# GpSimd forms the low part of one weight piece during the pool mixer, and VectorE leaves that split out

## The reference

```python
h = modulate(rms_norm(x, norm_g[i, 1]), sh1, sc1)
y = pool_mixer(h, pool_w, pool_scale)       # window means minus h, times a 256x256 matrix per group
x = x + g1 * y
h = modulate(rms_norm(x, norm_g[i, 2]), sh2, sc2)
x = x + 0.5 * g2 * swiglu(h, ffn_w_gu[i, 1], ffn_w_down[i, 1])
```

## Time and profile before

| | |
|---|---|
| median of 3 runs | 1389.89 us (1388.96 to 1390.38) |
| the profiled execution | 1388.13 us |
| its span | 1386.5 us |
| TensorE matmuls, busy | 1328.2 us, 96% of the span |
| VectorE busy | 946.5 us, 68% |
| ScalarE busy | 643.6 us, 46% |
| GpSimd busy | 150.5 us, 11% |
| VectorE's splits of pieces (L1890) | 212, mean 2293 ns |
| mean granted clock of TensorE | 0.988 of full |

### The profile page before, as it was taken

The page is one execution under the profiler, slowest core; times in us unless marked ns, Lnnn a source line. Parts: engine busy times, 40 slices in busy tenths (PEclk is TensorE's granted clock), DMA queues, the critical chain, the costliest instruction groups (busy, mean ns, idle before and its releaser), DMA issues.

```text
span 1386.5 us, 17673 instructions
## 1 busy us (share of the span) xinstructions
PE 1328.2 (96%) x6207; PEld 1080.6 (78%) x6207; DVE 946.5 (68%) x1125; ACT 643.6 (46%) x845; POOL 150.5 (11%) x215
## 2 busy tenths in 40 slices
PE   5999999799999999999998899999999999999997
PEld 2678888688888888888787678888887777888886
DVE  3788888779887788887576566465786556554442
ACT  3344334543333743335566553433655663644341
POOL 2110001200010100000331100010126000000000
PEclk9999999999999999999999999999999999999999
DMA  9899887499896799874532385565346444365540
GB/s 334 297 351 333 304 304 265 143 333 310 304 310 212 244 305 310 306 248 146 200 122 92 121 290 174 192 193 204 125 165 204 154 151 136 123 219 189 196 154 31
DMA packets 179926, 304.82 MB, mean 220 GB/s; under 512 B 8524, under 2 KB 122596, under 8 KB 179608
## 3 DMA queue, kind: packets, MB, share of 16 engines
q1 hardware_dynamic: 159288, 224.63, 48.1%
q0 software_dynamic: 20576, 79.37, 16.3%
HBM read 302.91 MB, written 1.05 MB: 219 GB/s over the span
## 4 chain that ended last, share of the span: by engine, by line
PE 46%; ACT 3%; DVE 2%; issue 1%; POOL 1%; POOLq 0%; DVEq 0%; ACTq 0%
PE ps L501 14%; PE ps L503 14%; PE ps L502 14%; ACT whi L1275 1%; PE ps L944 1%; PE ps L583 1%; PE ps L924 0%; PE ps L656 0%; DVE wlo L1890 0%; PE ps L1056 0%; PE ps L933 0%; POOL xn L2833 0%; PE ps L1172 0%; PE ps L592 0%; PE ps L914 0%
## 5 line engine op out<-in xcount | busy, mean ns | idle before, releaser
L1890 DVE TENSOR_TENSOR wlo<-raw,whi 128x2048 fp32r<-128x2048 f32 x212 | 481.2, 2293 | 97.5 <-ACT whi L1275 95.3
L501 PE MATMUL ps<-whi,nthi 128*128 128x512 f32 (+1 forms) x1264 | 508.9, 403 | 9.5 <-DVE ntlo L2214 6.6
L503 PE MATMUL ps<-whi,ntlo 128*128 128x512 f32 (+1 forms) x1264 | 495.9, 392 | 0.0
L502 PE MATMUL ps<-wlo,nthi 128*128 128x512 f32 (+1 forms) x1264 | 495.4, 392 | 0.0
L1275 ACT ACTIVATE whi<-raw 128x2048 fp32r<-128x2048 f32 x212 | 396.9, 1909 | 71.4 <-DMA raw<-in_ffn_w_gu 28.0
L501 PEld LDWEIGHTS ps<-whi,nthi 128*128 128x128 f32 x1264 | 240.5, 190 | 58.9 <-issue 8.6
L503 PEld LDWEIGHTS ps<-whi,ntlo 128*128 128x128 f32 x1264 | 239.8, 190 | 51.6
L502 PEld LDWEIGHTS ps<-wlo,nthi 128*128 128x128 f32 x1264 | 240.5, 190 | 45.5
L1931 DVE SCALAR_TENSOR_TENSOR arena<-arena,cact 128x512 f32<-128x512 f32 x238 | 178.8, 751 | 10.5 <-DMA arena<-in_mod_w 2.9
L501 PE MATMUL ps<-whi,hthi 128*128 128x512 f32 x440 | 172.9, 393 | 1.2 <-DVE htlo L1981 1.0
L503 PE MATMUL ps<-whi,htlo 128*128 128x512 f32 x440 | 171.8, 390 | 0.0
(11 more groups left out here) (265 smaller groups left out, 859.1 us busy)
## 6 DMA issues: line engine op xcount, KB each, us to landing
raw<-in_ffn_w_gu SPq DMA_DIRECT2D x176, 512.0 KB, 5.3
arena<-in_mod_w POOLq DMA_DIRECT2D x72, 1024.0 KB, 7.0
raw<-in_ffn_w_down SPq DMA_DIRECT2D x88, 512.0 KB, 5.7
raw<-in_w_in SPq DMA_DIRECT2D x44, 512.0 KB, 4.5
raw<-in_w_gate_up SPq DMA_DIRECT2D x44, 512.0 KB, 4.8
raw<-in_diff_w_qkv SPq DMA_DIRECT2D x24, 512.0 KB, 4.5
raw<-in_w_down SPq DMA_DIRECT2D x22, 512.0 KB, 5.9
raw<-in_diff_w_o SPq DMA_DIRECT2D x8, 512.0 KB, 4.0
```

The lines of the kernel that those rows point to most:

```text
L501: pe.matmul(o, hi, wh, start=start, stop=False)
L502: pe.matmul(o, hi, wl, start=False, stop=False)
L503: return pe.matmul(o, lo, wh, start=False, stop=stop)
L1890: v.tensor_tensor(wlo[:, s * PIECE:(s + 1) * PIECE], raw[:, r * PIECE:(r + 1) * PIECE], hi, ALU.subtract).then_inc(w_lo, 1)
```

## The change

VectorE's `split(1)` at the head of `pool_join` is left out. GpSimd forms the same tile with the same subtraction, in its queue behind the two DMA issues in the mixer and ahead of the next row scale. It waits until the high part of piece 34 is made and the low part of piece 33, so that `w_lo` is counted in order. VectorE counts the piece as passed and waits for it ahead of its split of piece 35.

```diff
--- before.py
+++ after.py
@@ -2224,9 +2224,10 @@
 
                 dve.wait_ge(rstd_done, n.next("rstd").at + 1)
                 n.next("rstd")
-                split(1)
                 first_half(0, j, scol[:, :], shift)
                 x_lo(0)
+                n.next("piece")
+                dve.wait_ge(w_lo, START["ffn1"] + 2)
                 split(3)
                 return j, (scol[:, :], shift)
 
@@ -2890,6 +2891,12 @@
             rms(turn=False)
 
             load_chunk(*MOD_HEAD[1], behind=1)
+            piece = START["ffn1"]
+            pool.wait_ge(w_hi, piece + 2)
+            pool.wait_ge(w_lo, piece + 1)
+            s, r = piece % RING, piece % RAW
+            g.tensor_tensor(wlo[:, s * PIECE:(s + 1) * PIECE], raw[:, r * PIECE:(r + 1) * PIECE],
+                            whi[:, s * PIECE:(s + 1) * PIECE].bitcast(F32), ALU.subtract).then_inc(w_lo, 1)
             skip(a=1, b=1, t=1, m=3)
             join()
 
```

## The result

Over 20 runs each, the changed kernel takes 1390.62 us (median) against 1388.93 us for the kernel before; the ratio is 1.0022, 95% interval 1.0012 to 1.0031. So it is slower by 1.7 to 4.3 us. The medians are 1.69 us apart (0.12%), the means 2.9 us: four of the 20 runs of the changed kernel took 1394.8 to 1397.7 us, at a granted clock of 0.982 to 0.984, and none of the kernel before but one far outlier at 3215.85 us lies above 1391.2. The forecast was 1391.8 us, made from a median before of 1389.89 and +1.89 us. The median lies 1.2 us under it, of which 0.96 us are the kernel before, which ran at 1388.93 here. "Within 0.2%" had 67% and "slower by over 0.2%" 30%: the medians fall in the first, the ratio of 0.22% just in the second, and its interval has both. The profiled execution took 1389.93 us (span 1388.3), 1.80 us more than the one before.

What follows compares the result with a forecast made beforehand. The second FFN's start was taken as bound by TensorE's 3.7 us wait for VectorE's low part. A +2.55 us delay in the mixer less 0.66 us removed gave +1.89, from 1389.89 to 1391.8 us, range 1389.1 to 1393.9.

Steps and rivals of the forecast that it cites:

- What bounds the kernel: Second FFN: TensorE waits 3.7 us for VectorE's low part, then runs matmul to matmul, so delays there reach the end.
- What is removed: Ahead of the second FFN: 2.29 us of VectorE's split go, but only 0.66 us count, as ScalarE's half is late next.
- GpSimd's length: GpSimd's new subtraction in the mixer: 4.58 us for 2048 columns, estimated from shorter operations, bounds 2.29 and 5.85 us.
- The hold: Mixer: VectorE's first `mixed_lo`, with two SBUF inputs, must wait until GpSimd's subtraction ends, +2.55 us; `mix` goes on as before.
- The load of piece 37 and the moved wait: Piece 37 loads earlier, at about 254.6 instead of 265.25 us, and VectorE waits for `w_lo` before later splits; counted as 0.
- The sum: Whole program: +2.55 us of delay less 0.66 us removed gives +1.89 us, forecast 1391.8 us.
- TensorE's clock: Gap before the second FFN: slow clock costs nine matmuls 1.83 us, and gap and loss stay; a mixer fall might add 0.8 to 1.8.
- the clock falls in the mixer too: Rival: TensorE's clock also drops in the mixer's new stall, +1.89 + 1.5 = +3.4 us, 1393.3 us; 17%.
- `mix` held: Rival: in the mixer VectorE's `mix` must wait for GpSimd as well, +3.7 us, 1393.6 us; 7%.
- GpSimd slower: Rival: GpSimd's subtraction in the mixer needs over 5.5 us, +2.8 us and more, about 1393.5 us; 6%.
- nothing held: Rival: `mixed_lo` in the mixer does not wait for GpSimd, only the -0.66 us is left, 1389.2 us; 9%.

Runs made afterwards that it cites:

- e2: Kernel before with VectorE's split of piece 34 left out and done by nobody; mean -0.6 ± 0.5 us against the kernel before, ratio 0.9997.
- e3: Kernel before plus GpSimd's subtraction, with VectorE still doing its own split; mean +3.7 ± 0.8 us against the kernel before, ratio 1.0034.
- e5: Changed kernel with GpSimd's subtraction done twice, the second waiting for the first; mean +7.1 ± 0.8 us against the kernel before, ratio 1.0047.
- e1: Changed kernel run again without edit; mean +3.9 ± 0.7 us against the kernel before, ratio 1.0030.
- e12: Changed kernel run a third time without edit; mean +3.0 ± 0.6 us against the kernel before, ratio 1.0022.
- e9: Kernel before with VectorE's split of piece 34 moved right ahead of the first `mixed_lo`, GpSimd doing nothing new; mean +3.3 ± 0.7 us, ratio 1.0027.
- e7: Changed kernel with 16 more matmuls on TensorE in the stall before the mixer's first group; mean +3.1 ± 0.6 us against the kernel before, ratio 1.0020.
- e4: Kernel before with piece 34 shared: GpSimd 1408 columns ahead of its DMA issues, VectorE 640 at the old place; mean +0.9 ± 0.7 us, ratio 1.0010.
- e8: Kernel before with piece 34 shared: GpSimd 1024 columns ahead of its DMA issues, VectorE 1024 at the old place; mean -0.1 ± 0.5 us, ratio 1.0001.
- e10: Kernel before with VectorE splitting piece 34 in two halves, one in its idle time in the mixer, without GpSimd; mean -0.3 ± 0.5 us, ratio 0.9996.
- e11: Kernel before run again without edit, as a control; mean -0.2 ± 0.6 us against the kernel before's other runs, ratio 0.9998.

## Why the prediction was right, point by point

- **What bounds the kernel: right, with one wait overlooked.** What is late at the FFN's start is late behind it: path +1.60, +1.71 at 453 us and +1.70 at 762. But TensorE does not run from matmul to matmul throughout the FFN. The wait of 0.54 us at 316.25, a second one of over half a microsecond, takes in what the slow clock adds to the path.
- **What is removed: right, 0.66 us forecast, 0.78 measured** (4.98 - 4.20; 0.77 by the path of e2). ScalarE's half was named as what is late next, and it is. The 0.12 us between are those by which ScalarE starts its next instruction before the row of the last one ends: 266.76 - 265.38 = 1.38, for an instruction group of 1.50.
- **GpSimd's length: right**, 4.58 forecast, 4.53 measured, 3.18 for 1408 and 2.35 for 1024 columns. The estimate from two short shapes held over 8 times their size. The figure of the Trainium skill (4497 ns for an add of this shape, GPSIMD Engine Reference, section 3.1) holds as well.
- **The hold: right, 2.55 forecast, 2.36 measured.** The held instruction is through 0.56 us after GpSimd rather than 0.69; e3 has it alone and e5 twice. `mix`, which reads one input from PSUM, was never held. The rule of the Trainium skill (SBUF — State Buffer, section "SBUF: two separate sides") is borne out as far as these traces reach: the operation with two SBUF inputs waits (0.69 to 3.05 us) and `mix` does not (1.79 us in both), the wait lasts for the whole instruction, and whichever engine starts first goes on.
- **The load of piece 37 and the moved wait: right,** counted as 0. The path of the changed kernel is e3's part and e2's part added: +2.37 - 0.77 = +1.60, with nothing left for them.
- **The sum: right on the path, too low for the mean.** Forecast +1.89, path +1.60, +1.71 at 453 us, medians +1.69 apart in the first set. But the means are +2.9 to +3.9 over three sets of runs (44 runs, mean +3.2), and the later medians are further apart as well (1391.56 against 1387.60 in e1, 1390.84 against 1387.24 in e12). So that the first median fell so near is in part luck.
- **TensorE's clock: the loss was mis-sized.** The forecast was that the gap stays and 1.83 us of loss with it. The slow time stayed at 6.8 us, but the shorter gap and the later fall put more of it on matmuls. Before, nine matmuls ran slow, 3.87 us; after, twelve, 273.52 - 268.27 = 5.25, a loss of 5.25 - 12 x 0.227 = 2.5 us instead of 1.8. In e12, e9 and e3 the transposes were slow too, another 0.7. So the long path is +2.3, +2.3 and +2.9 in the three traces of the changed kernel. That is near the means but does not explain them, as 0.5 to 0.7 us of it are gone at 453 us.
- **The rival "the clock falls in the mixer too"** did not come true in any trace of the changed kernel. That its sum, +3.4 us, lies near the mean of +3.2 is a coincidence as far as the traces show. e7 speaks against the mixer's stall as the place of the loss.
- **The other rivals** (`mix` held, GpSimd slower, nothing held) are out by the traces.

What is shown, then, is the hold and its 1.6 to 1.7 us. What the mean has above that is not: 1.3 us (3.2 less the 1.9 by which the three traces are late at 453 us), with a standard error of about 0.4. The same traces are 3.0 to 3.6 us late at the end, as much as the means, but the 1.2 to 1.4 us that come in between are there in the traces of e2, e4, e8 and e10 too (1.5 to 1.6 us), and of these kernels only e4 has a mean above the kernel before, by 0.9 ± 0.7. The cause of the surplus stays open.

## What to carry to other kernels

In these runs, work given to GpSimd was free only where no VectorE instruction with two SBUF inputs came due before it was over: look at the inputs of what VectorE has queued there, and set the whole length of GpSimd's instruction against the first of them. A half of the same work, earlier, cost nothing; the whole of it, 0.9 us earlier, still cost 1.44. Before moving work off an engine, see who is late next: of 2.29 us removed, 0.77 counted, and half of the split moved into that engine's own idle time gave the same. Where a gap of TensorE moves or shrinks, look at how much of the slow time then falls on matmuls: here that added 0.7 us. And follow a delay on to the next wait: 0.6 us of this one ended there.

## What the runs showed of the hardware that was not expected

- GpSimd and VectorE alternate: in e5 the waiting VectorE instruction came in between GpSimd's two, which stood 0.1 us apart, and the second of GpSimd's took 4.86 us instead of 4.54. So the hold was paid twice.
- The time before the mark varies from trace to trace of the same kernel: 247.84 and 245.19 us for the kernel before, 246.66, 246.72 and 245.26 for the changed one. A single pair of profiled executions could not have shown the change; marks inside the trace repeat to 0.03 us (path 20.01 and 20.02, 21.61 and 21.59) as long as the clock is the same.
- In the attention (660 to 781 us) both traces of the kernel before lack a slow stretch that all twelve others have, whatever their edit; in e1 it lies before 707 us, in the others behind 762. TensorE from 763 to 766 us in e11 and in e2:

```profile
763.00:766.00 3.00, 3.00 (x20) 1.00 0.74 209
```

```profile
763.00:766.00 3.00, 3.00 (x14) 0.50 0.56 166
```

It costs 1.4 us in e1 and 2.7 to 2.9 in the others, of which 1.5 to 1.6 come back by 973 us in all but e1. e2, e8 and e10 have it too, and their mean times are not above those of before, so a stretch like this cannot by itself be the surplus. Nor can it be ruled out as a part of it, since each trace is one execution. Why it is missing from just these two traces stays open.
